# The last two expert pairs of layer two in both arms of TensorE's test for further slot rounds

## What is computed

```python
def hier_moe_2(xn, wg, bg, we, be, w_gate, w_up, w_down):
    ...
    weights = g_top_p * jax.nn.softmax(top_val, axis=-1)
    expert_id = grp[:, None] * MOE_EXPERTS_PER_GROUP + top_idx
    ...
    def expert_block(args):
        xblk, e = args
        h = jax.nn.silu(xblk @ w_gate[e]) * (xblk @ w_up[e])
        return h @ w_down[e]
    ...
    y = jnp.zeros((T + 1, D), f32).at[buf_tok].add(yb.astype(f32) * buf_w[:, None])[:T]
```

## Time and profile before

| what | before |
|---|---|
| median of 3 runs (lowest, highest) | 991.95 us (991.24, 992.96) |
| profiled execution, its own time | 991.52 us |
| its span, first to last instruction | 989.8 us |
| TensorE busy | 919.8 us, 93% of the span |
| VectorE, ScalarE busy | 307.0 us, 207.3 us |
| DMA moved | 339.80 MB, mean 343 GB/s |
| granted TensorE clock, mean | 0.99 |

### The profile page before, as it was taken

How to read it: one execution, slowest core, us unless ns; L and a number is a source line. 1 busy time by engine, 2 the same in 40 slices (tenths; PEclk the granted TensorE clock), 3 DMA queues, 4 the chain that set the end, 5 groups by cost and what they waited for, 6 DMA issues and landing times.

```text
span 989.8 us, 11796 instructions
## 1 busy us (share of the span) xinstructions
PE 919.8 (93%) x4653; PEld 493.9 (50%) x4653; DVE 307.0 (31%) x664; ACT 207.3 (21%) x440; POOL 23.3 (2%) x61
## 2 busy tenths in 40 slices
PE   8999999999999998999999999998888888889886
PEld 5777475555655555866447433333333333333332
DVE  3356366333332334132126132222111122101213
ACT  3232353221121114024323021111011111011112
POOL 4001300000000000000000000000000000000000
PEclk9999999999999998999999999999999999999998
DMA  9950546999999999635456999999999999999994
GB/s 318 388 175 4 209 149 248 422 422 421 419 421 420 421 420 387 245 137 170 154 209 232 396 413 380 401 426 430 426 431 427 430 428 427 431 425 427 420 420 201
DMA packets 53970, 339.80 MB, mean 343 GB/s; under 512 B 9917, under 2 KB 10961, under 8 KB 24610
## 3 DMA queue, kind: packets, MB, share of 16 engines
q1 hardware_dynamic: 48048, 337.59, 84.1%
q10 hardware_dynamic: 5458, 1.39, 0.6%
q0 software_dynamic: 416, 0.16, 0.1%
HBM read 338.07 MB, written 1.05 MB: 343 GB/s over the span
## 4 chain that ended last, share of the span: by engine, by line
PE 69%; DMA 22%; DVE 5%; ACT 1%; issue 1%; SPq 0%; DVEq 0%; ACTq 0%
PE ps L1156 23%; PE ps L1220 12%; DMA ring<-in_expert_w_down_dram 11%; DMA ring<-in_expert_w_gate_dram 9%; PE ps L2269 8%; PE ps L2418 5%; PE ps L1239 4%; PE ps L2483 4%; DMA ring<-in_w_up_dram 2%; PE ps L2257 1%; PE ps L1062 1%; PE ps L1579 1%; PE ps L1381 1%; PE ps L1194 1%; PE ps L2393 1%
## 5 line engine op out<-in xcount | busy, mean ns | idle before, releaser
L1156 PE MATMUL ps<-ring,work 128*64 128x256 f32 (+1 forms) x2040 | 339.1, 486 | 20.7 <-DMA ring<-in_expert_w_up_dram 10.5
L1156 PEld LDWEIGHTS ps<-ring,work 128*64 128x64 f32 x2040 | 153.0, 137 | 199.0 <-issue 162.9
L1220 PE MATMUL ps<-ring,work 128*64 128x512 f32 x696 | 159.6, 602 | 9.2 <-DMA ring<-in_expert_w_down_dram 8.0
L913 DVE TENSOR_TENSOR work<-work,ps 128x256 f32<-128x256 f32 (+1 forms) x30 | 16.4, 545 | 273.5 <-PE ps L1156 273.5
L1220 PEld LDWEIGHTS ps<-ring,work 128*64 128x64 f32 x696 | 52.0, 138 | 96.9 <-issue 86.1
L2269 PE MATMUL ps<-xT,ring 128*128 128x256 f32 (+1 forms) x384 | 86.0, 382 | 0.0
L1239 PE MATMUL ps<-parts 128*128 128x512 f32 x248 | 73.7, 419 | 6.6 <-DVE parts L934 6.6
L2269 PEld LDWEIGHTS ps<-xT,ring 128*128 128x128 f32 x384 | 72.3, 191 | 11.3 <-issue 1.2
L1239 PEld LDWEIGHTS ps<-parts 128*128 128x128 f32 x248 | 41.9, 189 | 41.8 <-DVE parts L934 18.5
L741 ACT ACTIVATE work<-ps,small 128x512 f32<-128x512 f32 x30 | 20.6, 687 | 188.4 <-PE ps L1220 188.4
L2418 PE MATMUL ps<-ring,work 128*128 128x512 f32 x128 | 56.0, 595 | 2.2 <-ACT work L1905 1.8
(11 more groups left out here) (392 smaller groups left out, 687.2 us busy)
## 6 DMA issues: line engine op xcount, KB each, us to landing
ring<-in_expert_w_gate_dram SPq DMA_DIRECT2D x20, 2048.0 KB, 17.1
ring<-in_expert_w_up_dram SPq DMA_DIRECT2D x20, 2048.0 KB, 17.6
ring<-in_expert_w_down_dram SPq DMA_DIRECT2D x20, 2048.0 KB, 17.7
ring<-in_w_gate_dram SPq DMA_DIRECT2D x32, 1024.0 KB, 17.4
ring<-in_w_up_dram SPq DMA_DIRECT2D x32, 1024.0 KB, 18.9
ring<-in_w_down_dram SPq DMA_DIRECT2D x32, 1024.0 KB, 16.3
ring<-in_expert_w_up_dram SPq DMA_DIRECT2D x24, 1024.0 KB, 12.6
ring<-in_expert_w_gate_dram SPq DMA_DIRECT2D x23, 1024.0 KB, 11.9
```

Of the source, the lines that this page charges most:

```text
L1156: mm = pe.matmul(ps[CAP * e:CAP * e + CAP, 4 + which, 0:ff], slots, chunks[e][:, k, :], start=(k0 + k == 0), stop=(k0 + k == KC - 1), skip ...
L1220: mm = pe.matmul(ps[CAP * e:CAP * e + CAP, 6 + half, :], hT[:, c0 + k, CAP * e:CAP * e + CAP], columns(chunks[e], k, half), start=(c0 + k ...
```

## The change

In layer one nothing is changed but that the body of the test stands in a function. In layer two the test is turned round: where there are no further rounds (extra < 1), last_two follows at once; in the Else arm stand the further rounds and a second copy of last_two. The instructions of either path are the same as before, but for the branches: before, the path without further rounds takes the branch over the rounds' code; after, it falls through the compare and takes a branch over the Else arm at its end. The other engines are not touched.

```diff
@@ -1424,7 +1424,9 @@
 
             pe.wait_ge(ev("rounds"), TURN[tag])
             extra, earlier_x = extra_rounds(pe, tag)
-            with pe.If(extra > 0):
+
+            def more_rounds():
+
                 with pe.Fori(0, extra) as r:
                     with pe.Fori(0, PAIRS) as q:
                         n = earlier_x * 2 + (r * PAIRS + q)
@@ -1445,8 +1447,16 @@
                         for half in range(2):
                             mm = scatter(n, half, False, True, "_x")
                         mm.then_inc(ev("experts_summed"), 1)
-            if tag == "m2":
-                last_two(EARLIER[tag] + LAST_A)
+
+            if tag == "m1":
+                with pe.If(extra > 0):
+                    more_rounds()
+            else:
+                with pe.If(extra < 1):
+                    last_two(EARLIER[tag] + LAST_A)
+                with pe.Else():
+                    more_rounds()
+                    last_two(EARLIER[tag] + LAST_A)
```

## The result

| | before | changed |
|---|---|---|
| median of 19 runs (lowest, highest) | 991.61 us (990.49, 993.26) | 993.63 us (991.98, 995.58) |
| profiled execution: time, span | 991.52, 989.8 | 993.42, 991.7 |

The ratio is 1.0018, with a 95% interval of 1.0011 to 1.0024: slower by 1.1 to 2.4 us. The forecast of 991.9 us with a range up to 993.4 missed it by 0.2 us at the upper end, and its likeliest case (nothing to be seen) was wrong.

The account below looks back on a forecast made before the run. Weight transfers over the DMA engines were taken to bound the tail. The 0.37 us won at the test given back, fetches 0 and the end jump hidden left a span of 989.8 and a median of 991.9 us, range 990.6 to 993.4.

Parts of the forecast that it names:

- What bounds the tail: After the layer-two test, weight transfers set the pace; 0.37 us won there is given back at two transfer waits.
- One of the signs named for being wrong: Any change ahead of 928.7 us, where the instructions are the same, would show the prediction wrong.
- The test itself: TensorE's layer-two compare falls through in 80 ns instead of 445, so TensorE restarts 0.37 us earlier.
- Rival 1: Tail paced by TensorE, so the compare's gain reaches the end: 991.6 us, or 990.5 with the fetch saved; chance 0.07.
- rival 2: The layer-two compare costs 445 ns in either direction, so time stays 991.95 us; chance 0.09.
- Instruction fetches in the tail: One TensorE code fetch fewer between 928.7 and 976.4 us; worth 0 to 1.1 us, taken as 0.
- The new jump at the end: TensorE's jump over the Else arm, from 981.9 us, is hidden by 7.7 us of cover; 5 us if fully waited for.
- rival 3: TensorE's end jump outlasts SP's drain at 989.6 us; two full fetches, 10 us, give 994.3 us; chance 0.06.
- Rival 4: A late 16 KB code fetch holds up one output by up to 1.1 us: 993.0 us; chance 0.12.
- the third bullet: The end-jump step: the Else arm's further rounds and 217 matmuls with weight loads are at least two 16 KB code packets.
- The rule cited there: At the end jump: a taken branch whose target lies outside the two code pages held must wait for a fetch.
- Base: Whole kernel's starting median, 991.95 us; the profiled execution's 991.52 lies 0.43 below it.

Follow-up runs that it names:

- 1.16 us of added work in the experiment: Kernel before with four idle 128x128 matmuls added between the layer-two jump and last_two; ratio 1.0004 (0.9995 to 1.0013).
- the old test and an end jump: Kernel before, old test kept, plus a second test behind last_two jumping over dead code as long as the Else arm; ratio 1.0014 to the kernel before.
- 1.9 us late in the experiment: Changed kernel with TensorE waiting ahead of its end jump until VectorE has made the last quarter of the result; ratio 1.0012 to the kernel before.
- The second and third comparison: The unaltered changed kernel run twice more beside the kernel before on the same chip; ratios 1.0013 and 1.0011.
- the changed kernel again: The unaltered changed kernel, second comparison and trace, against the kernel before; ratio 1.0013 (1.0004 to 1.0022).
- the short Else arm: Changed kernel whose Else arm holds only the further rounds, without the second copy of last_two; ratio 1.0001 (0.9992 to 1.0010) to the kernel before.
- the kernel without a test: No TensorE test or further-rounds code in layer two, last_two follows at once; ratio 1.0004 (0.9995 to 1.0013) to the kernel before.

## Why the prediction was wrong, point by point

- *What bounds the tail.* Right. The waits for the up transfers took up the 0.36 us in the changed kernel, and 1.16 us of added work in the experiment. One of the signs named for being wrong did come, a change ahead of 928.7 us (0.41 us), and both restarts were 0.66 and 0.79 us late. But the same scatter matmuls start at 927.77, 928.02 and 927.07 us in the changed kernel's three traces, the last ahead of the 927.36 of before, so this is scatter between executions, which the prediction hadn't measured.
- *The test itself.* Right: 80 ns assumed, 83 measured. The idle time fell by 0.36 us, 0.37 was worked out. Rival 1 (the gain reaches the end) and rival 2 (the compare costs the same either way) are out.
- *Instruction fetches in the tail.* Right in number: one q8 packet between 928.7 and 976.4 us in place of two. No gain came of it that could be seen, as taken.
- *The new jump at the end.* Here the prediction failed, in the step "a span of 989.8 again, end jump hidden". Its cover was counted for TensorE's sequencer alone: 7.7 us against a jump that took 3.3 to 3.6 us, so rival 3, with TensorE last at the barrier, didn't come, rightly. What wasn't covered was the DMA engine that brings the code.
- *Rival 4* (a late fetch meets the outputs) is the case that came, with a chance of 0.12 given to it. Two of its terms were mis-sized. The time of the fetch was taken from the old jump, 3.9 us behind it, one page; in the runs there were two pages, the first 1.0 us behind the jump and the second 0.8 us behind its end, 4.4 us after its start, in the first trace (0.7 to 1.8 us behind its end in all of them). The text said that it decides from a fetch that still runs 3.4 us after the jump starts, and the third bullet had counted at least two pages: put together, the second page lay past that point. And the price was bounded by a page's own 1.1 us, while the output stage grew by 1.1, 0.9 and 2.1 us in three traces of the changed kernel (0.9 with the old test and an end jump), and one landing was 1.9 us late in the experiment. The sum had the engine away for the page's packet alone; by the packets' times it is away from the outputs from their start until the page is in. The mean of the three, 1.4 us, is a ratio of 1.0014, inside the intervals of all three comparisons.
- *The rule cited there* from the Trainium skill ("Runtime: NRT & Kernel Launch", Instruction fetch mechanics) agrees with these runs: the jump over one body of code took 0.31 us and the one over some three pages 3.3 to 3.6 us, and 4.5 us where its page came 1.1 us later. (Three pages is an estimate: last_two is 217 matmuls and 217 weight loads, a body about half of that, and 234 such instructions ran between two packets where no jump is the earlier trace rows.) That it may load the DMA engines for others isn't in that rule; the traces show it.
- *Base.* The kernel before was 991.95 in 3 runs and 991.61 in 19. The absolute forecast lay 0.3 us high by that, which hid as much of the miss: from 991.61 the same working gives a miss of 2.0 us.

What stays open: whether 2.0 us (the first comparison's medians) holds anything besides the output stage. The second and third comparison say 1.3 and 1.1 us by their ratios, and nothing ahead of the stage could be told from scatter. Why the engine leaves the outputs alone up to a microsecond before the page's packet starts, why the second page comes 0.7 or 0.8 us behind the jump's end in three traces and 1.2 to 1.8 us in three others, and why SP's issue waits for a page, no run here shows. No version here beats the kernel before: all that can be won at the test is absorbed.

## What to carry to other kernels

A branch that is taken can cost more than its engine's time. Here, when the target lay some three pages off, pages of code came over a DMA engine that the outputs needed too, and the output stage grew by 0.9 to 2.1 us; the same jump behind the outputs did them no harm. So look at what a long jump at the end of a program passes, and whether outputs follow it. The short jump in the middle, where TensorE waits for weights anyway, was free with its 0.36 us; a long one of 3.5 us was not tried there, and it is more than the 2.1 us of waits (1.32 and 0.75 us) that are there to take it up. And when a wait is declared hidden, ask for each resource it uses, the DMA engines too, who else needs it in those microseconds.

## What was not expected of the hardware

- A jump of TensorE over some three pages of code takes 3.3 to 3.6 us with the DMA nearly idle, and 4.5 us with outputs under way; over one body 0.24 to 0.46 us, both layers and all runs taken together.
- A long jump brings two pages: one 0.9 to 1.2 us behind its start (2.2 with outputs under way), for which it waits, and one 0.7 to 1.8 us behind its end (behind the span's end where the jump itself came last).
- With a single 16 KB code page under way an output issue on SP went from 0.33 to 0.43 us to as much as 1.54 us (the changed kernel again), and in other executions one output's landing from 2.7 to 4.6 and 4.8 us.
- In three traces the outputs end 2.8 to 2.9 us behind the second page's end, the time that all of them take without a page: one DMA engine of 16 gives them nothing until the page is in.
- A page that came ahead of the outputs' own packets did nothing: at 983.06 with the short Else arm, and at 984.60 in the kernel without a test. The stage was 4.0 us in both.
